# Eight blocks of squares summed by one strided DVE pass before a single ones-product, in the channel normalisations of a hybrid decoder step

## The reference, cut to what matters

```python
def rms_norm(x, g):
    xf = x.astype(jnp.float32)
    y = xf * lax.rsqrt(jnp.mean(xf * xf, axis=-1, keepdims=True) + RMS_EPS)
    return (y * g.astype(jnp.float32)).astype(x.dtype)
...
proj = rms_norm(xp, norm_mix_g[l]) @ w_in[l]
...
mn = rms_norm(mem, g_mem)
k = rms_norm((mn @ w_k).reshape(bn, m, M_HEADS, M_HD), k_g)
...
q = rms_norm((rms_norm(x, g_x) @ w_q).reshape(bn, t, M_HEADS, M_HD), q_g)
...
h = jnp.square(jax.nn.relu(rms_norm(x, g_f) @ w1))
```

## Time and profile before

| what | value |
|---|---|
| median of 3 runs | 3831.97 us (3829.27 to 3839.28) |
| the profiled execution, its own time | 3828.85 us |
| its span, first to last instruction | 3826.6 us |
| PE busy | 2981.0 us, 78% of the span |
| DVE busy | 1216.7 us, 32% |
| ACT busy | 746.1 us, 19% |
| mean granted TensorE clock | 0.862 of full speed |

### The profile page before, as it was taken

The page is one execution under the profiler, slowest core; times in us unless marked ns, Lnnn a source line. Parts: engine busy times, 40 slices in busy tenths (PEclk is TensorE's granted clock), DMA queues, the critical chain, the costliest instruction groups (busy, mean ns, idle before and its releaser), DMA issues. The chain is left out here.

```text
span 3826.6 us, 49559 instructions
## 1 busy us (share of the span) xinstructions
PE 2981.0 (78%) x21754; PEld 2544.9 (67%) x21754; DVE 1216.7 (32%) x2017; ACT 746.1 (19%) x1102; POOL 105.0 (3%) x144
## 2 busy tenths in 40 slices
PE   4994888655874378959669999674665699999998
PEld 3982787524871245536558888573553599999998
DVE  3346444242014255623311111223331422222222
ACT  2122221000111134421101111112121222222222
POOL 0000221000000000001000000000000000000000
PEclk8986999567995589978879999886877899999999
DMA  4300000003112200025241111201003011111111
GB/s 161 106 14 1 3 3 3 13 14 113 35 28 77 17 1 1 1 76 203 103 151 42 42 42 44 79 22 56 22 0 105 22 50 45 50 45 45 50 45 57
DMA packets 205349, 190.14 MB, mean 50 GB/s; under 512 B 48372, under 2 KB 189879, under 8 KB 199646
## 3 DMA queue, kind: packets, MB, share of 16 engines
q1 hardware_dynamic: 167441, 118.33, 10.6%
q0 software_dynamic: 5760, 68.16, 4.5%
q10 hardware_dynamic: 31934, 0.49, 0.5%
HBM read 164.34 MB, written 26.95 MB: 50 GB/s over the span
## 5 line engine op out<-in xcount | busy, mean ns | idle before, releaser
L410 PE MATMUL ps<-xf_h,ff_high 128*128 128x352 f32 x768 | 248.9, 324 | 22.7 <-DVE ff_low L399 22.7
L2937 PE MATMUL ps<-ff_hidden_high,ff_high 128*128 128x352 f32 x768 | 249.3, 325 | 4.8 <-issue 4.8
L2938 PE MATMUL ps<-ff_hidden_low,ff_high 128*128 128x352 f32 x768 | 249.2, 324 | 0.0
L2939 PE MATMUL ps<-ff_hidden_high,ff_low 128*128 128x352 f32 x768 | 249.1, 324 | 0.0
L412 PE MATMUL ps<-xf_h,ff_low 128*128 128x352 f32 x768 | 247.5, 322 | 0.0
L411 PE MATMUL ps<-xf_l,ff_high 128*128 128x352 f32 x768 | 247.4, 322 | 0.0
L410 PE MATMUL ps<-xn_h,pj_high 128*128 128x352 f32 x528 | 174.8, 331 | 74.8 <-DVE pj_low L399 74.8
L410 PE MATMUL ps<-xn_h,me_high 128*128 128x352 f32 x576 | 192.7, 335 | 33.3 <-DVE me_low L399 33.3
L411 PE MATMUL ps<-xn_l,me_high 128*128 128x352 f32 x576 | 185.3, 322 | 0.0
L412 PE MATMUL ps<-xn_h,me_low 128*128 128x352 f32 x576 | 185.3, 322 | 0.0
L411 PE MATMUL ps<-xn_l,pj_high 128*128 128x352 f32 x528 | 172.9, 327 | 0.0
(11 more groups left out here) (640 smaller groups left out, 6213.7 us busy)
## 6 DMA issues: line engine op xcount, KB each, us to landing
ff_raw<-in_w_ff SPq DMA_DIRECT2D x64, 512.0 KB, 4.0
me_raw<-in_w_in SPq DMA_DIRECT2D x24, 512.0 KB, 4.2
pj_raw<-in_w_in SPq DMA_DIRECT2D x21, 512.0 KB, 4.8
xn_h<-xn_high POOLq DMA_DIRECT2D x2, 4224.0 KB
xn_l<-xn_low POOLq DMA_DIRECT2D x2, 4224.0 KB
x_channel_major<-xT POOLq DMA_DIRECT2D x1, 4224.0 KB, 13.5
xn_high<-xn_h POOLq DMA_DIRECT2D x1, 4224.0 KB, 14.9
xn_low<-xn_l POOLq DMA_DIRECT2D x1, 4224.0 KB, 24.6
```

What stands on the lines that cost most here:

```text
L410: e.matmul(o, W.hi[:, z, k, :], rh[:, k, n], start=k == ks[0], stop=False)
L2937: e.matmul(o, W.hi[:, u % NSPL, 2 * k + z, :], hh[:, r, ns], start=k == 0, stop=False)
L2938: e.matmul(o, W.hi[:, u % NSPL, 2 * k + z, :], hl[:, r, ns], start=False, stop=False)
L2939: mm = e.matmul(o, W.lo[:, u % NSPL, 2 * k + z, :], hh[:, r, ns], start=False, stop=k == GB - 1)
```

## The change

A tile `part` of [128, 2, w] and a semaphore `_partial_sums` are added to `stage_rms`. DVE now sums the eight blocks of squares of a chunk by one `tensor_reduce`. Its input is `sq` read through a view whose innermost dimension is the block, so successive elements are w * 4 bytes apart; its output is w sums for each partition. PE then makes one product with the ones instead of eight. The reduce of chunk 0 stands at the head of DVE's list; that of chunk c+1 stands behind the drain that signals `_normed` of chunk c, and ahead of DVE's wait for `hi` and of the subtraction that makes `lo`.

```diff
         sq = ctx.enter_context(nc.sbuf_tensor(name + "_sq", [P, 2, KD, w], F32))
         rstd = ctx.enter_context(nc.sbuf_tensor(name + "_rstd", [P, 2, w], F32))
+        part = ctx.enter_context(nc.sbuf_tensor(name + "_partial", [P, 2, w], F32))
...
+        s_part = K.sem(name + "_partial_sums")
...
         @block.tensor
         def _(e):
             for c in range(nchunk):
+                e.wait_ge(s_part, c + 1)
+                if c >= 2:
+                    e.wait_ge(s_var, c - 1)
+                e.matmul(K.ps[:, c % 2, 0:w], K.c("ones"), part[:, c % 2, :], start=True, stop=True).then_inc(s_sum, 1)
+
+        @block.vector
+        def _(e):
+            def partial(c):
                 e.wait_ge(s_sq, c + 1)
                 if c >= 2:
-                    e.wait_ge(s_var, c - 1)
-                for k in range(KD):
-                    mm = e.matmul(K.ps[:, c % 2, 0:w], K.c("ones"), sq[:, c % 2, k, :], start=k == 0, stop=k == KD - 1)
-                mm.then_inc(s_sum, 1)
-
-        @block.vector
-        def _(e):
+                    e.wait_ge(s_sum, c - 1)
+                e.tensor_reduce(part[:, c % 2, :], sq[:, c % 2, :, :].rearrange("p k n -> p n k"), AX.X, ALU.add).then_inc(s_part, 1)
+
+            partial(0)
             for c in range(nchunk):
                 e.wait_ge(s_sum, c + 1)
                 e.tensor_scalar(rstd[:, c % 2, :], K.ps[:, c % 2, 0:w], 1.0 / D, RMS_EPS,
...
                 e.drain().then_inc(s_nrm, 1)
+                if c + 1 < nchunk:
+                    partial(c + 1)
                 e.wait_ge(s_hi, c + 1)
```

## The result

| what | before | after |
|---|---|---|
| median | 3832.11 us (13 runs) | 3845.39 us (3839.29 to 3855.51, 13 runs) |
| ratio, with its 95% interval | | 1.0034 [1.0024, 1.0044] |
| profiled execution, span | 3826.6 us | 3849.3 us |

What follows compares the result with a forecast made beforehand. The prediction took each normalisation stage as a chain through DVE and ACT, with PE's products on the path only in first chunks. Terms of -3.6 and +13.1 us made +9.5 on 3831.97, so 3841.5 us, range 3824 to 3853.

Steps and rivals of the forecast that it cites:

- The place of the products: In the normalisation stages, PE's eight products delay the scaling only in the first chunk, by 6.36 to 7.61 us.
- The price of the reduce: On DVE, each strided reduce takes 4.87 us, or 3.58 in "mem", including 0.63 ns an element for the step.
- The first rival: In DVE's reduces, the step costs nothing: 3.09 us each, net -7.8 us, kernel 3824.2 us; chance 15%.
- the second: In DVE's reduces, the step costs a whole second slot: 6.02 us each, net +20.7 us, kernel 3852.7 us; chance 22%.
- First chunks: In each stage's first chunk, a reduce and one product replace eight products on the path: 3.6 us saved in all.
- The later reduces: In second and third chunks, six times, the reduce delays `lo` by 2.19 us beyond the wait for `hi`: 13.1 us lost.
- The sum: Over the whole kernel, -3.6 and +13.1 us make +9.5 us, forecast 3841.5 us, 0.25% more.
- the middle case: In DVE's reduces, a duration between 4.8 and 5.1 us, sum +9 to +11.7 us, kernel 3837 to 3846; chance 60%.
- The 0.3% line: For the whole kernel, the smallest difference a measurement can tell from no change: about 0.3%, 11.5 us.
- The clock: Behind the stages, PE might come slower to the following product; priced at nothing, chance 3% with anything else.

Runs made afterwards that it cites:

- first-only reduce: Changed kernel with reduce and single product in each stage's first chunk only, eight products kept in later chunks: 3836.66 us, ratio 1.0011; timed again 3831.29 us, ratio 0.9995.
- the probe: Kernel before plus a stage of thirteen 512-element DVE operations at various steps: reduces took 0.69 us at 4 and 8 bytes, 1.01 to 1.07 from 16.
- e1_adjacent: Changed kernel with each reduce reading the same 2816 squares at adjacent addresses, summing other elements than wanted: 3824.51 us, ratio 0.9979.
- before's second profile: Kernel before, unchanged, profiled again: span 3830.7 us, four stages 166.8 us, "mem" 17.4 us.
- the repeats: Second profiles of the kernel before and of the changed kernel, both unchanged: spans 3830.7 and 3845.4 us.
- delay kernel: Kernel before with one extra strided reduce on DVE behind the last `lo` of "mix" and of "ffn", all products kept: 3845.38 us, ratio 1.0027.

## Why the prediction was right, point by point

- **The place of the products.** As the prediction had it: on the path in the first chunk of a stage only, beside DVE's work in the others. Exchanging eight products for a reduce and one product in the first chunks bought 3.6 us in all (first-only reduce, against the first profile of before).
- **The price of the reduce.** Forecast 4.87 us, and 3.58 in "mem"; measured 4.88 and 3.59 in the first chunks and 4.97 in the later ones. L2566 and L2569, two rows of another stage, gave the first chunks' to 0.01 us. That this is so close is in part luck: L1208, the row with two strided inputs, would have given 5.03, and in the probe the step costs between 0.63 and 0.74 ns an element at 16 bytes or more. The first rival (3.09 us, the step costs nothing) and the second (6.02 us) are both out; `e1_adjacent` shows what the first would have given: 0.9979, forecast as 3824.2 us and measured as 3824.5.
- **First chunks.** Forecast 3.6 us saved; measured 0.22 us in "mix" (6.73 - 6.51), and 3.6 us over the four stages. Both are counted against the profile that the forecast was read from. Against the other profiles that keep the products it is 1.6 to 5.2 us: the forecast took the products' time from one execution, and this time isn't constant. The largest term, the 1.5 us of "mem", would be 0.3 us by before's second profile.
- **The later reduces.** Forecast 2.19 us each and 13.1 us in all; measured 2.39 us (the period from scaling to scaling is 15.62 us in the mean of the six, 13.23 before) and 14.4 us. This term was 1.2 us too small: behind the normalising instructions a reduce takes 4.97 us, not 4.88, and starts 0.12 us on instead of 0.05 (0.19 in the second of a stage).
- **The sum.** Forecast +9.5 us and 3841.5 us; the stages show +10.7 and, in the repeats, +11.3, and the median is 3845.4 us, +13.0 by the ratio (9.2 to 16.9). The stated range, 3824 to 3853, has the two rivals as its ends; the middle case alone (3837 to 3846) holds the result near its upper end. Of the 3.5 us missing in the sum, 1.2 are the later reduces. The difference of 2 us between stages and median lies in the interval and in the scatter of the stages of before; no run shows a cause for it.
- **The 0.3% line.** The forecast sum lay 2 us below it, and 0.54 was put on "same", 0.42 on "slower". The measured ratio lies just above it, with the line inside its interval. The two cases were that close, as the prediction said.
- **The clock.** Forecast: no price. The one product ran at 1.54 us, as forecast, and nothing waited for it in the later chunks. What follows did not come out slower: the stretches behind the last three stages together are those of before within 1.5 us. A window over "mix" in the changed kernel shows a granted clock of 0.50, the level of 1.2 GHz, for the stage, where before it was 0.74:

```profile
33.00:86.70 53.70, 4.62 (x6) 1.50 (x6) 44.54 (x36) 17.82 (x10) 0.68 (x1) 0.50 0.19 81
```

## What to carry to other kernels

Before moving a sum from PE to DVE, look whether PE's products are on the path at all, chunk by chunk: here they were in 4 of 10, and the other six paid for DVE time on an engine that was the chain. A reduce over a transposed view is priced by its addresses: 1.7 to 1.8 ns an element from 16 bytes of step on, against 1.04 for adjacent ones; a few adjacent additions that halve the data do the same sum in 3.2 us instead of 4.9. And rows of another stage with the same pattern of addresses are worth looking for: they gave the price in advance. A time of PE's products read from one profile is one draw: here it moved by up to 1.7 us in a stage.

## What was not expected of the hardware

- A copy with a step of 64 bytes takes 0.59 us for 512 elements, where an addition or a reduce with the same step takes 1.01 to 1.02; adjacent it takes 0.43. The copy's price for the step is 0.16 us, half of theirs. Why isn't shown.
- The same reduce takes 4.88 us in the first chunks and 4.97 to 4.98 us in the later ones. That it follows right behind other DVE work is not the reason: in the delay kernel it starts 0.1 us behind `lo` and takes 4.88. Only the later ones run while ACT makes `hi` (49.72 to 52.27 in "mix"). No run separates this from other causes, and the adjacent reduces at the same place stay at 3.09 us.
- The RWKV stage, unchanged code, took 333.9 to 343.5 us from one profile to the next, as its granted clock was 0.92 to 0.89. Two medians of a dozen runs of one kernel lay 5.4 us (0.14%) apart; a difference of this size in this kernel isn't settled by a median. The stages help, within limits: their sum repeats to 0.02 us where PE has one product in the first chunk, and moved from 165.3 to 167.7 us where it has eight.
